# A two-layer block chain in one kernel: modulation weights transposed and summed along rows on VectorE, the opening by eight slices of input channels

## The reference

```python
def ada_mod(c, w, b, n):
    h = jax.nn.silu(c) @ w + b
    return jnp.split(h[:, None, :], n, axis=-1)

def gmlp_layer(x, c, ada_w, ada_b, norm_g, w_in, sgu_g, w_s, b_s, w_out):
    shift, scale, gate = ada_mod(c, ada_w, ada_b, 3)
    h = rms_norm(x, norm_g) * (1 + scale) + shift
    u, v, z = jnp.split(h @ w_in, 3, axis=-1)
    u = jax.nn.gelu(u)
    v = rms_norm(jax.nn.gelu(v), sgu_g)
    ...
    y = u * mixed.reshape(bsz, s, A_WIDTH) * jax.nn.silu(z)
    return x + gate * (y @ w_out)
```

## Time and profile before

| | us |
|---|---|
| runs listed | 1620.35, 1623.29, 1874.79 |
| median | 1623.29 |
| span of the profiled execution (its own time is not listed apart; the lowest run is 1620.35) | 1618.4 |
| PE busy in the span | 1535.2 |
| DVE busy | 1030.4 |
| ACT busy | 589.4 |
| POOL busy | 209.6 |

### The profile page before, as it was taken

One profiled execution on the slowest core, in us unless ns is written; L12 is line 12 of the kernel. 1 busy time (PEld: TensorE's weight loads), 2 busy tenths in 40 slices (PEclk: granted clock), 3 DMA queues, 4 the chain that ended last, 5 costly groups with the idle time before them and its releaser, 6 DMA issues.

```text
span 1618.4 us, 20739 instructions
## 1 busy us (share of the span) xinstructions
PE 1535.2 (95%) x7736; PEld 1246.4 (77%) x7736; DVE 1030.4 (64%) x1616; ACT 589.4 (36%) x824; POOL 209.6 (13%) x79
## 2 busy tenths in 40 slices
PE   7899999999899899999999799999988999999999
PEld 6899888888678677777777566766656788888887
DVE  4866788876699578777786726677664533432343
ACT  2323322232254344444443354455543322321131
POOL 1100000101010222222213222222113000000000
PEclk9999999999989999999999899999998999999999
DMA  8454445545435222222222111111002222223212
GB/s 359 157 182 160 178 156 181 180 173 208 156 104 183 79 78 79 79 78 78 78 105 98 58 53 53 36 69 52 27 27 78 78 104 104 81 101 104 100 69 91
DMA packets 26139, 178.44 MB, mean 110 GB/s; under 512 B 3040, under 2 KB 3296, under 8 KB 5344
## 3 DMA queue, kind: packets, MB, share of 16 engines
q1 hardware_dynamic: 25200, 175.22, 30.0%
q10 hardware_dynamic: 880, 2.41, 0.4%
HBM read 175.52 MB, written 2.10 MB: 110 GB/s over the span
## 4 chain that ended last, share of the span: by engine, by line
PE 84%; DVE 12%; issue 2%; ACT 1%; DMA 1%; POOL 0%; SPq 0%; DVEq 0%; ACTq 0%; POOLq 0%
PE acc L1256 72%; PE ada L1256 5%; PE turn L1256 3%; PE norm L1256 2%; DVE ada_acc L768 2%; DVE ada_acc L780 2%; PE turn L1503 1%; PE turn L1623 1%; DVE s L1149 1%; DVE s_b L768 1%; DMA ada_up<-in_ada 1%; DVE y_half L768 1%; DVE h_lo L768 1%; DVE rstd L768 1%; DVE s L1166 0%
## 5 line engine op out<-in xcount | busy, mean ns | idle before, releaser
L1256 PE MATMUL acc<-h_hi,w_hi 128*128 128x512 f32 x992 | 407.1, 410 | 12.0 <-DVE h_lo L768 8.6
L1256 PE MATMUL acc<-h_hi,w_lo 128*128 128x512 f32 x992 | 388.8, 392 | 0.0
L1256 PE MATMUL acc<-h_lo,w_hi 128*128 128x512 f32 x992 | 388.5, 392 | 0.0
L426 ACT ACTIVATE w_hi<-w_raw 128x2048 fp32r<-128x2048 f32 (+1 forms) x108 | 204.4, 1893 | 119.0 <-PE acc L1256 119.0
L1256 PEld LDWEIGHTS acc<-h_hi,w_hi 128*128 128x128 f32 x992 | 187.5, 189 | 64.4 <-issue 18.9
L374 POOL TENSOR_TENSOR w_lo<-w_raw,w_hi 128x2048 fp32r<-128x2048 f32 x33 | 151.3, 4584 | 599.1 <-ACT w_hi L426 583.0
L1256 PEld LDWEIGHTS acc<-h_lo,w_hi 128*128 128x128 f32 x992 | 187.6, 189 | 43.7 <-issue 7.2
L775 DVE TENSOR_TENSOR w_lo<-w_raw,w_hi 128x2048 fp32r<-128x2048 f32 (+1 forms) x75 | 171.8, 2290 | 76.5 <-ACT w_hi L426 76.4
L1256 PEld LDWEIGHTS acc<-h_hi,w_lo 128*128 128x128 f32 x992 | 187.3, 189 | 40.6
L768 DVE SCALAR_TENSOR_TENSOR ada_acc<-ada_raw,silu_c,ada_acc 128x256 f32<-128x256 f32 x336 | 164.0, 488 | 12.0
L1256 PE MATMUL acc<-w_hi,h_hi 128*128 128x256 f32 x368 | 107.7, 293 | 6.4 <-DVE h_lo L768 6.4
(11 more groups left out here) (203 smaller groups left out, 2550.0 us busy)
## 6 DMA issues: line engine op xcount, KB each, us to landing
w_raw<-in_weights SPq DMA_DIRECT2D x104, 1024.0 KB, 4.7
ada_raw<-in_ada SPq DMA_DIRECT2D x48, 1024.0 KB, 4.8
ada_up<-in_ada SPq DMA_DIRECT2D x8, 1024.0 KB, 20.4
w_raw<-in_weights SPq DMA_DIRECT2D x4, 768.0 KB, 3.9
x<-in_x SPq DMA_DIRECT2D x2, 1024.0 KB, 16.4
out<-x SPq DMA_DIRECT2D x8, 256.0 KB, 2.0
consts<-in_tiles ACTq DMA_DIRECT2D x1, 590.0 KB, 4.2
blocks<-in_blocks ACTq DMA_DIRECT2D x1, 576.0 KB, 3.5
```

The costliest lines, as they stand in the source:

```text
L426: nc.scalar.activation(w_hi[par][:, 0:used], w_raw[par][:, 0:used], ACT.Copy).then_inc(hi_done, 1)
L1256: return nc.tensor.matmul(out, lhsT, rhs, start=start, stop=stop)
```

## The change

The modulation weights are stored transposed: one unit is 128 output columns on the partitions and the 1024 input channels along the free axis (0.5 MB). silu(c) and silu(c_2) are spread over all partitions as rows (csil), by four PE products of a row of ones with c and a Silu on ACT. A unit is then one DVE instruction, product and row sum (accum_out) straight into a column of mods. PE's sums over partitions (`ada_sum_up`) are gone. Biases are added in two large steps. Of the 112 units 16 belong to the opening; the others are spread 4 per chunk over V, 2 per chunk over u/z and 4 per chunk over the output of layer A; none remain in K/V, heads or output B. Two buffers ada_raw of 0.5 MB are used.

The opening goes by eight slices: slice kt has the unit of shift and of scale for tile kt (one DMA of 1 MB), its bias add and gscale column, all on DVE; POOL scales x by 1/rms (x_scale), ACT makes h_hi and h_full, POOL subtracts h_lo (first_lo). PE makes chunks 0 and 1 side by side, 24 products per tile. The first chunks are loaded before ada_up 1 to 7. ws_t is loaded late and masked by DVE behind v_stat.

```diff
             def ada_load(k, i, par):
...
-                ge(sp, ada_sum, 8 * r)
-                sp.dma_start(ada_raw[:, :, :].rearrange("p k n -> p (k n)"), src).then_inc(ada_loaded, 16)
+                ge(sp, ada_done, k - 1)
+                sp.dma_start(ada_raw[par][:, :], src).then_inc(ada_loaded[par], 16)
...
+            sp.dma_start(c_in[0:1, 0:DM], d["c"]).then_inc(c_loaded, 16)
+            sp.dma_start(c_in[0:1, DM:2 * DM], d["c_2"]).then_inc(c_loaded, 16)
             sp.dma_start(vecs[:, :], d["vecs"]).then_inc(vecs_loaded, 16)
-            for s in range(3):
-                ada_up_load(s)
+            ada_up_load(0)
             for half in range(2):
                 sp.dma_start(x[:, 4 * half:4 * half + 4, :], d["x"][:, 4 * half:4 * half + 4, :]).then_inc(x_loaded[half], 16)
-            for s in range(3, UP):
-                ada_up_load(s)
             for par in range(2):
                 load(W_V // 2, par)
+            for s in range(1, KT):
+                ada_up_load(s)
...
+            with sp.Fori(W_OUTA // 2 + 1, W_KV // 2 + 1) as u:
+                for par in range(2):
+                    load(u, par)
+                    ada_loads(FIRST_OUT_UNIT + 2 * UNITS_OUT * (u - W_OUTA // 2 - 1) + UNITS_OUT * par,
...
+            nc.gpsimd.memset(one_row[:, :], 1.0).then_inc(one_ready, 1)
             sum_squares(0, sq_first[0][:, :], lambda m: sq_first[m][:, :])
             to_lo(0, 1)
+            pool.wait_ge(rstd_done, N_X0 + 1)
+            for kt in range(1, KT):
+                x_scale(kt)
+                first_lo(kt - 1)
+            first_lo(KT - 1)
...
+            for n in range(4):
+                act.wait_ge(c_spread_in, n + 1)
+                nc.scalar.activation(csil[n // 2][:, TOK * (n % 2):TOK * (n % 2) + TOK], G[n][:, :], ACT.Silu).then_inc(csil_ready, 1)
             act.preload_act_table_set("natural_log_exp_and_others")
...
+            to_hi(0, 0)
             rstd_start(N_X0, NB[:, :], DM)
+            to_hi(0, 1)
             act.wait_ge(lam_part, 2)
             nc.scalar.activation(lam_two[:, :], lam_two[:, :], ACT.Exp).then_inc(lam_exp, 1)
-            to_hi(0, 0)
-            to_hi(0, 1)
-            h_round(0, SHIFT_A, False)
+            for kt in range(KT):
...
+                act.wait_ge(gsa_done, kt + 1)
+                shift, gain = mods[:, SHIFT_A + 2 * kt:SHIFT_A + 2 * kt + 1], gscale[:, kt:kt + 1]
+                nc.scalar.activation(h_hi[:, kt, :], x_n[:, kt, :], ACT.Identity, bias=shift, scale=gain).then_inc(hhi_done, 1)
+                nc.scalar.activation(h_full[:, kt, :], x_n[:, kt, :], ACT.Identity, bias=shift, scale=gain).then_inc(hx_done, 1)
+
+            act.dma_start(ws_t[:, :, :], d["spatial"]).then_inc(ws_loaded, 16)
...
+            def ada_unit(k, i, par, cond):
+
+                dve.wait_ge(ada_loaded[par], 16 * (i + 1))
+                stt(ada_raw[par][:, :], ada_raw[par][:, :], 1.0, csil[cond][:, :], ALU.mult, ALU.mult,
+                    accum_out=mods[:, bass.ds(k + FIRST_MODS, 1)]).then_inc(ada_done, 1)
...
+            def up_unit(kt):
+
+                dve.wait_ge(ada_up_loaded[kt], 16)
+                for e in range(2):
+                    stt(ada_up[kt][:, e, :], ada_up[kt][:, e, :], 1.0, csil[0][:, :], ALU.mult, ALU.mult,
+                        accum_out=mods[:, 2 * kt + e:2 * kt + e + 1]).then_inc(up_done, 1)
+                dve.wait_ge(up_done, 2 * kt + 2)
+                pair = slice(2 * kt, 2 * kt + 2)
+                nc.vector.tensor_tensor(mods[:, pair], mods[:, pair], mod_bias[:, pair], ALU.add).then_inc(up_out, 1)
+                dve.wait_ge(up_out, kt + 1)
+                stt(gscale[:, kt:kt + 1], mods[:, SCALE_A + 2 * kt:SCALE_A + 2 * kt + 1], 1.0, vecs[:, G_A + kt:G_A + kt + 1],
+                    ALU.add, ALU.mult).then_inc(gsa_done, 1)
...
+            to_lo(0, 0)
             rstd_end(N_X0, NB[:, :], DM, x_rstd)
+            nc.vector.tensor_tensor(x_n[:, 0, :], x[:, 0, :], x_rstd[:, :], ALU.mult).then_inc(xn_first, 1)
+            for kt in range(1, KT):
+                up_unit(kt)
...
-                    ada(n + par, 0)
+                    ada(UNITS_V * (n + par), UNITS_V // 2 * (n + par), UNITS_V, 0)
...
-                    ada(j + W_UZ, 0)
+                    ada(FIRST_UZ_UNIT + UNITS_UZ * j, FIRST_UZ_UNIT // 2 + UNITS_UZ // 2 * j, UNITS_UZ, cond)
...
+            dve.wait_ge(ws_loaded, 16)
+            dve.wait_ge(consts_loaded, 16)
+            tri = consts[:, K_TRI:K_TRI + P].unsqueeze(1).broadcast_to([P, GROUPS, P])
+            nc.vector.tensor_tensor(ws_t[:, :, :], ws_t[:, :, :], tri, ALU.mult).then_inc(ws_ready, 1)
...
-                    ada(m + W_OUTA, 8)
-                    dve.wait_ge(ada_out, m + W_OUTA)
+                    ada(FIRST_OUT_UNIT + UNITS_OUT * m, FIRST_OUT_UNIT // 2 + UNITS_OUT // 2 * m, UNITS_OUT, 1)
                     update_x(m, G[2 * par][:, :], GATE_A, 4 * u + 2 * par + 2, 2)
...
-                    ada(2 * u + par, 8)
...
-                    if project and r == 1:
-                        ada(n + S_B, 8, T1[:, 256:258])
...
-                if c % 2 == 0:
-                    ada(S_OUTB + c // 2, 8)
...
-            def ada_sum_up(r, columns=AD[:, 0:2]):
-
-                pe.wait_ge(ada_sum, 8 * r + 8)
-                ge(pe, ada_out, r)
-                mm(columns[:, 0:1], ada_acc[:, 0:P], ones[:, 0:1], True, True)
-                mm(columns[:, 1:2], ada_acc[:, P:2 * P], ones[:, 0:1], True, True).then_inc(ada_mm_done, 1)
...
+            pe.wait_ge(one_ready, 1)
+            pe.wait_ge(c_loaded, 32)
+            for n in range(4):
+                mm(G[n][:, :], one_row[:, :], c_in[:, TOK * n:TOK * n + TOK], True, True).then_inc(c_spread_in, 1)
...
+            pe.wait_ge(csil_ready, 4)
             for kt in range(KT):
                 h_ready(0, kt)
...
+                for par in range(2):
+                    if kt == 0:
+                        chunk_ready(0, par)
+                    for t in range(TB):
+                        last = rows(FIRST_V[par][t][:, 0:256], par, t, 0, 256, (kt,))
```

More of the change, by code:

```diff
@@ L126, in program @@
     off_ada = take(8 * KB)
-    ada_raw = at("ada_raw", [P, KT, 256], off_ada)
+    ada_raw = [at(f"ada_raw{s}", [P, DM], off_ada + 4 * KB * s) for s in range(2)]
     consts = at("consts", [P, NCONST], take(4 * NCONST))
@@ L337, in _ @@
             for par in range(2):
[L338 to L341 removed]
                 load(1, par)
[L343 to L344 removed]
+                ada_loads(UNITS_V * par, UNITS_V // 2 * par, UNITS_V)
+            with sp.Fori(2, W_UZ // 2 + 1) as u:
                 for par in range(2):
                     load(u, par)
[L347 to L348 removed]
+                    ada_loads(2 * UNITS_V * (u - 1) + UNITS_V * par, UNITS_V * (u - 1) + UNITS_V // 2 * par, UNITS_V)
@@ L349, in _ @@
+            with sp.Fori(W_UZ // 2 + 1, W_OUTA // 2 + 1) as u:
                 for par in range(2):
                     load(u, par)
-                ada_load(u + (S_B - W_B // 2 - 1))
-            for par in range(2):
-                load(W_OUTB // 2 + 1, par)
-                ada_load(S_OUTB + par)
+                    ada_loads(FIRST_UZ_UNIT + 2 * UNITS_UZ * (u - W_UZ // 2 - 1) + UNITS_UZ * par,
+                              FIRST_UZ_UNIT // 2 + UNITS_UZ * (u - W_UZ // 2 - 1) + UNITS_UZ // 2 * par, UNITS_UZ)
@@ L355, in _ @@
+            with sp.Fori(W_OUTA // 2 + 1, W_KV // 2 + 1) as u:
+                for par in range(2):
+                    load(u, par)
+                    ada_loads(FIRST_OUT_UNIT + 2 * UNITS_OUT * (u - W_OUTA // 2 - 1) + UNITS_OUT * par,
+                              FIRST_OUT_UNIT // 2 + UNITS_OUT * (u - W_OUTA // 2 - 1) + UNITS_OUT // 2 * par, UNITS_OUT)
+            with sp.Fori(W_KV // 2 + 1, W_Q2 // 2) as u:
+                for par in range(2):
+                    load(u, par)
             with sp.Fori(W_Q2 // 2, W_DN2 // 2) as u:
@@ L1567, in _, with output @@
             values(QH - 1, 1, 3)
-            def output(w0, hi, lo_kt, lo_made, rest, early, steps):
+            def output(w0, hi, lo_kt, lo_made, rest, early):
                 late = tuple(kt for kt in range(KT) if kt not in early)
@@ L1583, in output @@
                             last.then_inc(mm_done, 1)
-                            if (c, half) in steps:
-                                ada_sum_up(steps[c, half])
             pe.wait_ge(s_freed, 4 * QH)
-            output(W_OUTB, yb_hi, yb_lo_of, yblo_done, (7,), (0, 4), {(0, 0): S_OUTB - 1, (2, 0): S_OUTB})
-            ada_sum_up(S_END - 1)
+            output(W_OUTB, yb_hi, yb_lo_of, yblo_done, (7,), (0, 4))
             add_squares(2, N_X2)
```

266 lines of the change are left out of this document (107 added, 159 removed).

## The result

The changed kernel takes 1642.7 us (median of 1644.17, 1637.14, 1641.22, 1646.98), the kernel before 1622.6 beside it on the same chip: a ratio of 1.0128, 95% interval 1.0103 to 1.0153. One of the four executions of the kernel before, 1874.79, lies 15% above the others and is left out of the ratio. The changed kernel is 1.3% slower, less than the 2% named in the prediction, and 5.7 us outside the predicted range. The spans are 1618.4 and 1642.2: +23.8, where the sum of the prediction said +0.2.

A forecast was written before the change was run, and what follows sets the result against it. PE was taken as the bound, 84% of the chain, except in the opening. Terms from +10.0 to -14.1 summed to +0.2 on the span of 1618.4; with 4.9 to the median, 1623.5 us, range 1600 to 1637.

The forecast's parts named there:

- The product, 1.15 from start to start: DVE's 128x1024 modulation product with row sum was to take 1.15 us from start to start.
- Rival C: The modulation product costs more: 1633 us in all at 1.4 a product, 1667 at 2.2; chance 0.12.
- 1, the opening, +10.0: Opening: DVE and POOL take turns, chunk 2 starts 8.0 us later, and a lowered clock adds 2.0.
- 2, the sums, and V "covered": PE's column sums go: -2.0 us in V, -5.4 in u/z; DVE's products there fit under PE's time.
- 3, V to u/z, stall 5.7: Before u/z PE waits 5.7 us for the late ws_t and loses 2.5 by the clock: +8.2.
- 4, output A, +12.2: Output of layer A: late unit loads make DVE's closed loop the bound at 12.5 us a chunk: +12.2.
- 512 in 3.3: Output of layer A: a 512 KB modulation load was to land in 3.3 us.
- 5, K/V, heads, output B, -22.8: Without sums and modulation work there: K/V -1.7 and -2.3, head 0 -2.0, heads 1 to 7 -14.1, output B -2.7.
- Rival D: The heads give nothing back, the weights of r=3 being late for another reason: 1635 us; chance 0.05.
- "The rest is untouched": All stages not named in the forecast, the second block included, were to keep their time: 0 us.
- Rival B: Output of layer A: loads land within 2 us and PE stays the bound, 14.9 less, 1608.6 us; chance 0.09.

The follow-up runs named there:

- experiments 4 and 8: Changed kernel with the opening's POOL passes on DVE: 1639.1 us; the same plus chunk 1 rounded earlier, its w_lo on DVE, unit pairs interleaved: 1629.7 us.
- e11: Kernel before with 128 bytes left free ahead of x_rstd, moving its large tiles to offset 0 modulo 256: 1629.1 us, ratio 1.0043.
- e5: Changed kernel with 128 bytes left free ahead of x_rstd, no instruction changed: 1640.7 us, ratio 1.0105.
- e10: Changed kernel with four modulation buffers in V and output A, plus 128 bytes left free ahead of x_rstd: 1594.4 us, ratio 0.9828.
- e12: Changed kernel with four modulation buffers in V and output A, and every tile moved by 128 bytes: 1603.4 us, ratio 0.9884.
- experiment 2: Changed kernel with two of each chunk's four modulation units before the next w_lo, two behind, in V and output A: 1635.5 us, ratio 1.0071.

## Why the prediction was wrong, step by step

- **The product, 1.15 from start to start: right.** 1.14 to 1.15 wherever two follow each other and POOL is idle (88.51, 89.66, 90.80). Rival C is out with it. The measured time disagrees with the rule of the Trainium skill (Vector Engine (DVE) Microarchitecture Reference, section 7, Points that are easy to get wrong) that such an instruction runs at half throughput: an estimate by it is 2.2 for a product, and the row has 1.22.
- **1, the opening, +10.0: the number near, in part by luck.** Chunk 2 came 6.9 later, forecast 8.0. The collision with POOL is there as forecast, but slices took 4.67 and not 5.15, so PE was done 3.6 earlier. Against this DVE stood 4.64 for a unit's load where the term had 2.4 for all waits of four units (7.0 less 4 times 1.15), and PE's idle was 6.6 instead of 4.0, of which 3.1 go with four buffers. Two errors cancel, and the second is that of step 4. The clock behind the idle was at the lower of its two levels, 1.2 GHz, as assumed, and again behind the stall on ws_t (us, busy times of PE, PEld, DVE, ACT, POOL, PEclk, DMA share, GB/s):

```profile
171.50:177.20 5.70, 5.67 (x14) 4.47 (x15) 5.37 (x4) 1.53 (x2) 3.92 (x2) 0.53 0.30 82
...
82.90:88.00 5.10, 4.97 (x23) 4.98 (x24) 2.45 (x4) 0.00 (x0) 0.00 (x0) 0.50 0.52 149
```

  The mechanism, POOL's passes and DVE's taking turns, is what experiments 4 and 8 took away.
- **2, the sums, and V "covered": this failed.** DVE's chunk in V was to be 10.7 of PE's 11.6. With two waits for loads it was 12.0 to 13.4. The gain of u/z was there and somewhat larger, 7.4 with the clock's 2.1 taken out (the first chunk up to its mixing took 13.5, before 11.4). V's forecast gain of 2.0 was eaten by PE's waits of 2.2 for w_lo.
- **3, V to u/z, stall 5.7: the size failed, with step 2's.** It was 14.0. With four buffers it is 5.0. The clock behind it, forecast 2.5, cost 2.1.
- **4, output A, +12.2: the mechanism was right, the landing mis-sized.** A closed loop on DVE it is, and the update waits for units three and four. But "512 in 3.3" is the shortest landing; in the loop above the loads of units three and four took 3.7 and 4.6 to land and the units started 3.9 and 4.8 after their buffers were free, so the units took 8.3 instead of 7.0, and the loop 13.83 instead of 12.5. 7 times 1.33 is 9.3, the first update came 1.5 late, and 0.9 lie behind the last one. I had taken the median landings of larger transfers of the kernel before and scaled them; I should have laid the queue of one chunk out, the 1 MB of the next weights among it.
- **5, K/V, heads, output B, -22.8: right.** -24.8. Rival D is out.
- **"The rest is untouched": this failed.** The instructions were, the addresses weren't: 7.2 us by e11 (about 2 of them beside the clock), none of which any view of the kernel before could show; the diff's lists of tiles could.
- **Rival B** had the right place and the wrong lever: it asked that loads land within 2. They needn't; they must be issued a chunk ahead.

The misses by stage, 10.1 + 11.7 + 6.2, less the 4.4 by which u/z, K/V, heads and output B did better on balance, are the 23.6 between the forecast's +0.2 and the span's +23.8. The 2.2 of the second block between e5 (708.1) and before (705.9) aren't a price of the placement: e10, with the same placement, has 705.8, and the granted clock of 0.74 against 0.83 above lies just there.

## What to carry to other kernels

Work that waits for a load inside a closed loop of two engines is paid with every round; count, for each buffer, from the instruction that frees it to the one that needs it again, with what stands in front of it in the queue, and let the buffers reach one whole round ahead. A large transfer issued just ahead of a small one that is wanted sooner costs too: putting it behind gave back 17.8 of the time here, where the buffers gave 40.2. When a forecast comes out near, check its terms one by one: the opening's was near because two errors cancelled. When a change alters the list of tiles, compare the offsets of all the tiles behind it: here the 512-column products were shortest when the activation tile lay at the same offset modulo 256 as the weight chunks.

## What the runs showed of the hardware that was not expected

- A float32r product of 128x128 by 512 columns takes 389 ns when weights and moving tile have the same offset modulo 256 bytes, and 392 to 398 when they differ by 128 (e5, e11, e12): 1.9% of the gu stage, 6.6 ns for each of its 528. Products of 256 columns with the weight chunk moving showed no such price (283 with the same offset, 281 with different ones). Only the difference 128 was tried.
- A 512 KB load took 3.2 to 6.9 us to land in output A of experiment 2, and up to 19.0 in the changed kernel, where the longest were issued in the opening. In experiment 2 the unit whose load stood right behind 1 MB started 6.8 after its issue; in the changed kernel unit three started 3.9 after its buffer was free. Keeping more of them on their way made each slower (5.7 to 5.9) and the kernel faster.
- The summing SCALAR_TENSOR_TENSOR with two float32 inputs of SBUF runs at 1.15 us for 1024 columns from start to start, and takes turns with POOL like other two-input forms: one took 5.53 beside POOL's w_lo.
